# Another arena layout and another order of work ahead of the expert windows, in a two-layer decoder step

## The chip, the core and the metric

One core of one Trainium2 chip runs the whole step in one launch. The time is device microseconds of that core, from start to end of an execution. Three executions of the kernel before took 3319.91, 3323.1 and 3322.9 us.

## The reference, cut to what matters

512 prompt tokens and 8 new tokens, width 1024, go through two layers; all of it is float32.

```
layer 0: y = differential attention with ALiBi (8 heads; the 8 new tokens also see 2 cached pages each)
layer 1: y = gated short convolution
each layer: h = LN(alpha*h + y)
            q = h @ w_q; per head: scores against 2 x 128 keys, top 16 of each, top 16 of the 256 sums
            idx = 16 experts of 16384, g = softmax(top scores)      # 8 heads -> 128 experts per token
            a = u_tab[idx] . h;  h = LN(alpha*h + sum_k g*gelu(a) * v_tab[idx])
            h = h + sigmoid(h @ Wg) * (p @ Wp)
```

A token meets 128 experts in a layer. For a tile of 128 tokens one gather fetches, for each token, one expert's row of u and of v, 8 KB, so a gather is 1 MB, and there are 1040 of them (4 tiles of 128 and one short one, in two layers).

## The kernel before, in words

Each of the five engines runs its own program, written from one list of pieces of work that the class `Plan` makes; an engine's instructions stand in the order of that list, and nothing overtakes. First there is a long stretch without experts, the *lead*: queries and keys (L1538), the values (`v`, L1581), 32 units of scores and softmax (`score`, `weigh`, `w_turn`, `pv`), the attention of the new tokens over cached pages (`s_out`, `o_turn`), the norms of the heads (`ms0`, `rms0`, `ms1`, `rms1`), the output product (`mix`), the layer norm (`norm_a`, `norm_b`), its turn, the first query features (`pq`) and the routing of the first heads (`route`, four pieces for each head; the fourth writes the ids of 16 experts).

Then come windows, one for each tile of tokens: 32 steps of four experts. An expert passes from the gather (POOL, L912) into a slot of the arena, to its dot product (DVE, L1500), to the gate and the diagonal matrix (ACT, L1078 to L1088), to two additions into `acc` (PE, L1683), which free the slot. The arena has 11 slots of 8 KB per partition. What else is to be done (products, norms, the next tile's routing) is dealt out over the 32 steps by `window`, from a start step to an end step and by the numbers in COST. DVE and ACT do these pieces two half steps (BEHIND) later than PE.

Before the first gathers the arena holds the buffers of the attention. Slots 0 to 2 hold scores and softmax; slots 3 to 5 the values of the prompt and half of the attention's output (`oT_early`); 6 to 8 the new tokens' values and two pairs of cache pages (`kv_pages`); 9 and 10 the other half of the output, `s_rows` and `rstd8`. So POOL issues gathers 0 to 5 as soon as the ids are there, 6 to 8 once the last `s_out` is done, and 9 and 10 after the last `rms1` (L905 to L911).

Weights come as panels of 1 MB over SP's queue, in order, into two homes in turn; each waits until the panel before it in its home is used up. The pages of the cache come over POOL's queue, two pairs at a time, and a pair waits for the use of the one before it (`vpair_used`). The products of PE go through four banks; a product waits until its bank's last content was read. Pieces with `fence` wait for all banks.

## Time and profile before

| | |
|---|---|
| median of three executions | 3322.9 us (3319.91 to 3323.1) |
| the profiled execution | 3319.91 us, its span 3318.0 us |
| PE, DVE, ACT, POOL busy | 91%, 68%, 38%, 37% |
| moved by DMA | 1248.09 MB, 376 GB/s over the span |
| mean granted TensorE clock | 0.967 of 2.4 GHz |
| chain that ended last | PE 57%, DMA 16%, DVE 16% |

A stretch's row in the table of windows has the busy time of each engine with the number of its instructions, the granted clock of PE (1.00 is 2.4 GHz, 0.50 is 1.2 GHz), the busy share of the core's 16 DMA engines and what they moved. In rows of the timeline, what stands in brackets is the idle time ahead of the instruction and who ended it. The lead ends near 386 us, the first window runs to about 745 us, the second to about 1070 us.

### The profile page before, as it was taken

The page shows a single profiled execution, that of the slowest core. Times are in us where ns is not written, and L with a number is a line of the kernel's source. Part 1 is how long each engine was busy: PE and PEld are TensorE (multiplying, and loading weights), DVE is VectorE, ACT ScalarE, POOL GpSimd, SP SyncE. Part 2 cuts the span into 40 slices and gives each one's busy share as a digit, 9 for nine tenths or more (in the row PEclk, how much of TensorE's full clock was granted, in tenths as well). Part 3 has the DMA queues.
Part 4 walks back from the last instruction along what each step waited for, and adds up shares of the span by engine and source line. Part 5 has one row for each costly group of instructions (what it writes and reads, how often), then busy time and mean ns, then how long its engine had stood idle before and what let it go on. Part 6 is the DMA issues. An engine that isn't in the chain of part 4 may idle for free.

```text
span 3318.0 us, 33637 instructions
## 1 busy us (share of the span) xinstructions
PE 3010.6 (91%) x9426; PEld 1674.3 (50%) x9426; DVE 2250.1 (68%) x5801; ACT 1268.1 (38%) x3602; POOL 1241.6 (37%) x1100
## 2 busy tenths in 40 slices
PE   8998899789997899999898799999999788888888
PEld 7765555335563455654454355665455344443334
DVE  0653657877647877778768757764667888787454
ACT  0143333343423543333433464332434445435332
POOL 0100234443434334443344334444644435444431
PEclk9998799899999999999999899999999989999999
DMA  4513799999999999999899999999999999999997
GB/s 177 210 72 117 280 390 411 420 422 407 412 412 421 400 408 419 421 421 421 345 421 421 401 371 396 414 419 392 422 421 420 422 382 384 422 397 421 421 421 295
DMA packets 179819, 1248.09 MB, mean 376 GB/s; under 512 B 20087, under 2 KB 23415, under 8 KB 32433
## 3 DMA queue, kind: packets, MB, share of 16 engines
q0 software_dynamic: 156896, 1115.93, 82.2%
q1 hardware_dynamic: 22592, 128.97, 9.8%
q8 instruction: 75, 1.23, 0.1%
q10 hardware_dynamic: 144, 1.05, 0.1%
q14 instruction: 112, 0.91, 0.1%
HBM read 1239.41 MB, written 6.50 MB: 375 GB/s over the span
## 4 chain that ended last, share of the span: by engine, by line
PE 57%; DMA 16%; DVE 16%; ACT 4%; DVEq 3%; issue 3%; POOL 1%; ACTq 1%; POOLq 0%; SPq 0%
PE acc L1683 30%; DMA arena<-in_uv,idx 15%; PE bank L1709 10%; PE bank L1700 7%; DVE arena L1500 7%; PE bank L1538 3%; PE bank L1581 2%; DVEq L1408 2%; ACT diag L1088 1%; ACT L1072 1%; POOL arena L912 1%; DVE yb L1344 1%; DMA arena<-in_uv,small 1%; DVE ya L1343 1%; DVE ya L1354 1%
## 5 line engine op out<-in xcount | busy, mean ns | idle before, releaser
L1683 PE MATMUL acc<-arena,diag 128*128 128x512 f32 x4160 | 1935.0, 614 | 233.5 <-ACT diag L1088 228.4
L912 POOL DMA_INDIRECT arena<-in_uv,idx x1024 | 1194.5, 1166 | 1690.9 <-PE acc L1683 1560.5
L1500 DVE CUSTOM_DVE_ANT_0 arena<-arena,h 128x1024 f32<-128x1024 f32 x1024 | 1217.8, 1221 | 367.5 <-DMA arena<-in_uv,idx 364.4
L1683 PEld LDWEIGHTS acc<-arena,diag 128*128 128x128 f32 x4160 | 794.3, 196 | 1201.4 <-issue 840.9
L1078 ACT ACTIVATE act_w<-dots 128x2 f32<-128x2 f32 x520 | 105.3, 202 | 1382.9 <-DVE dots L1500 1382.3
L1088 ACT ACTIVATE diag<-cst,act_w 128x128 f32<-128x128 f32 x1040 | 370.0, 395 | 149.4 <-PE acc L1683 115.9
L1709 PE MATMUL bank<-hT,panel 128*128 128x264 f32 (+2 forms) x1792 | 403.4, 379 | 2.2 <-ACT hT L1045 2.2
L1709 PEld LDWEIGHTS bank<-hT,panel 128*128 128x128 f32 x1792 | 335.5, 190 | 97.6 <-issue 52.6
L1081 ACT ACTIVATE act_w<-act_w 128x1 f32<-128x1 f32 x1040 | 250.2, 287 | 43.4 <-issue 1.1
L1078 ACT ACT_TABLE_LOAD x128 | 164.2, 1283 | 1.6
L1700 PE MATMUL bank<-panel,hT 128*128 128x256 f32 (+1 forms) x576 | 131.8, 383 | 5.4 <-ACT hT L1045 5.4
L1700 PEld LDWEIGHTS bank<-panel,hT 128*128 128x128 f32 (+1 forms) x576 | 97.0, 170 | 49.0 <-issue 24.2
L1700 PE MATMUL bank<-panel,qT 128*128 128x256 f32 (+1 forms) x512 | 115.4, 379 | 0.0
L1700 PEld LDWEIGHTS bank<-panel,qT 128*128 128x128 f32 (+1 forms) x512 | 83.8, 165 | 38.6 <-issue 15.8
L1072 ACT ACT_TABLE_LOAD x80 | 102.6, 1283 | 1.4
L1337 DVE COPY yb<-tp 128x256 f32<-128x256 f32 x80 | 34.0, 425 | 97.7 <-PE tp L1667 92.7
L1415 DVE SCALAR_TENSOR_TENSOR h<-h,bank 128x256 f32<-128x256 f32 (+1 forms) x40 | 16.7, 419 | 106.3 <-PE bank L1700 104.9
L1500 DVE DVE_READ_ACCUMULATOR2_ANT dots<- 128x1 f32 x1040 | 85.1, 82 | 0.0
L1538 PE MATMUL bank<-keys,panel 128*128 128x256 f32 x256 | 60.9, 393 | 9.3 <-DMA panel<-in_panels 9.3
L1667 PEld LDWEIGHTS tp<-keys,qT 128*128 128x128 f32 (+1 forms) x320 | 43.3, 172 | 43.1 <-issue 42.0
L1053 ACT ACTIVATE qT<-bank 128x264 f32<-128x264 f32 (+2 forms) x68 | 24.8, 365 | 103.0 <-PE bank L1709 102.8
L1382 DVE TENSOR_TENSOR yb<-ya,cst 128x512 f32<-128x512 f32 x80 | 55.4, 693 | 11.4 <-issue 0.6
(201 smaller groups left out, 2169.1 us busy)
## 6 DMA issues: line engine op xcount, KB each, us to landing
panel<-in_panels SPq DMA_DIRECT2D x103, 1024.0 KB
arena<-in_uv,idx POOLq DMA_INDIRECT x1024
arena<-in_cache_k POOLq DMA_DIRECT2D x16, 512.0 KB, 5.5
arena<-in_cache_v POOLq DMA_DIRECT2D x16, 512.0 KB, 5.0
arena<-out_y_s POOLq DMA_DIRECT2D x8, 512.0 KB, 6.0
arena<-in_panels SPq DMA_DIRECT2D x4, 1024.0 KB, 8.1
lng<-in_ln SPq DMA_DIRECT2D x6, 512.0 KB
lnb<-in_ln SPq DMA_DIRECT2D x6, 512.0 KB
```

The lines of the kernel that those rows point to most:

```text
L912: nc.gpsimd.indirect_dma_start(uv[:, e % SLOTS_UV, :], None, uv_dram[layer], bass.IndirectOffsetOnAxis(ids[:, r:r + 1], 0)).then_inc(gathe ...
L1072: nc.scalar.activation(r_ex, r_tv, ACT.Exp, bias=r_nm, accum_out=r_sum).then_inc(gexp_done, 1)
L1078: nc.scalar.activation(act_w[:, 1, half, s], dots[:, half, s], ACT.Gelu).then_inc(gelu_done, 1)
L1081: nc.scalar.activation(act_w[:, 2, half, r:r + 1], act_w[:, 1, half, r:r + 1], ACT.Copy, scale=act_w[:, 0, half, r:r + 1])
L1088: nc.scalar.activation(diag[:, r % DIAGS, :], mask, ACT.Copy, scale=act_w[:, 2, half, r:r + 1]).then_inc(diag_ready, 1)
L1408: dve.drain()
L1500: V.tensor_tensor_reduce(uv[:, e % SLOTS_UV, 0:D], uv[:, e % SLOTS_UV, 0:D], x_rows, 1.0, 0.0, ALU.mult, ALU.add, dots[:, G % 2, r:r + 1]) ...
L1538: m = mm(pj[n % 2][:, PW + G_OFF[g]:PW + G_OFF[g] + G_W[g]], w[:, c, :], src[g][:, c, 0:G_W[g]], start=(c == 0), stop=(c == C - 1))
L1581: t = mm(product_of[0:m, 0:PW], src[group_of(x.b)][:, c, local(x.b):local(x.b) + m], w[:, c, :], start=(c == 0), stop=(c == C - 1))
L1683: m = mm(acc[:, half * 512:(half + 1) * 512], diag[:, r % DIAGS, :], uv[:, e % SLOTS_UV, D + half * 512:D + (half + 1) * 512], start=False ...
L1700: last = mm(bank[0:m, x.n % BANKS, 0:PW], src[:, c, local(x.b):local(x.b) + m], weights[:, c, :], start=(c == 0), stop=(c == chunks - 1))
L1709: last = mm(bank[:, x.n % BANKS, 0:width], w[:, c, :], hT[:, c, lo:lo + width], start=(c == 0), stop=(c == C - 1))
```

## The change

Four parts go together.

*Layout.* Slots 0 to 2 stay. Slots 3 and 4 now hold the late half of the output, `s_rows` and `rstd8`; all values, the early half of the output and the cache pages lie from slot 5 on. Gathers 0 to 2 need the ids alone, 3 and 4 wait for the last `rms1`, and 5 to 10 for the last product of the first `mix` (`last_mix`).

*Panels.* The third and fourth panel of the first `mix` get homes of their own in the room of the values, and are loaded once all sums of the attention and all stores of the values are done; they no longer wait for the first two panels.

*Order of the lead.* The key rows of the new tokens stand ahead of the first two products of values, and the fence moves to them. The second part of `s_out` comes one unit after the first instead of three units. `ms0` stands ahead of the last scores, without the Sqrt instruction that loaded the table early. The four `mix` products of tile 0 come together, `q[0:2]` and all of head 0's routing earlier; three `mix` products of tile 1 move to the end of the lead.

*Windows.* All of head 1's routing stands in the first window instead of three quarters of it in the lead. Heads 3 to 7 are dealt over steps 5 to 16 (before 5 to 20). The second group's `mix`, norm and turns move from the second window to steps 16 to 32 of the first, and its query features take steps 0 to 17 of the second window (before, both shared steps 0 to 23).

The diff, without the lines that only rename the value buffers:

```diff
--- before.py
+++ after.py
@@ -55,8 +55,7 @@
 FREE_AT_FIRST = 3
-HELD_BY_PAGES = 6
-HELD_BY_SAMPLE = 9
+FREE_NEXT = 5
@@ -151,7 +150,7 @@
-        once = {("pq", 0, 0): "queries"}
+        once = {("mix", 0, 2): "values0", ("mix", 0, 3): "values1", ("pq", 0, 0): "queries"}
         self.home, self.before, self.nth = [], [], []
@@ -181,8 +180,8 @@
         key_rows = [[product("k_rows", b=b, half=half) for half in range(2)] for b in range(BLOCKS)]
+        key_rows[TB][0].fence = True
         values = [[product("v", self.v_panels[p], p=p, b=b) for b in range(BLOCKS)] for p in range(4)]
-        values[0][0].fence = True
         score = [[product("score", u=u, half=c) for c in range(2)] for u in range(len(UNITS))]
@@ -202,8 +201,7 @@
         for b in range(TB):
-            if b >= 2:
-                fill[b - 1].append(values[0][b])
+            fill[b].append(values[0][b])
             for half in range(2):
@@ -214,11 +212,11 @@
         for k in range(4):
-            fill[24 + k + 2 * (k // 2)].append(out[k // 2][k % 2])
+            fill[25 + k].append(out[k // 2][k % 2])
         for k in range(2):
-            fill[24 + k] += square[2 * k:2 * k + 2]
-
-        lead = values[0][0:2] + key_rows[TB] + [Piece("s_new")]
+            fill[28 + k] += square[2 * k:2 * k + 2]
+
+        lead = key_rows[TB] + [Piece("s_new")]
         for t in range(len(UNITS) - 1):
@@ -391,7 +389,7 @@
         m1[0].fence = True
-        self.keys_after = m0[0].panel
+        self.keys_after = m0[2].panel
         a0, a1, c0, c1 = self.norm(0, GROUP_TILES[0], False, True)
@@ -399,30 +397,30 @@
         rms1 = [self.product(Piece("rms1", hd=hd)) for hd in range(HEADS)]
-        self.last_rms = rms1[-1]
+        self.last_mix, self.last_rms = m1[3], rms1[-1]
         self.ms0, self.ms1 = ms0, ms1
...
         roots = [Piece("root", i=g) for g in range(2)]
-        lead += score[31] + [weigh[30], turned[29], ms0, roots[0], turned[30], f0, weigh[31], summed[6, 1]] + rms0[0] \
-            + [turned[31], m0[0], summed[7, 1], m0[1], f1] + rms0[1] + [m1[0], o_turn[0], out[2][0], m1[1], out[2][1]] \
-            + [m0[2], m0[3], a0, m1[2], m1[3], c0] + t0 + q[0:2] + r[0:1] + q[2:4] + r[1:3] + out[3] + [o_turn[1]] + r[3:7] \
-            + [ms1, roots[1], f2] + rms1
+        lead += [ms0] + score[31] + [weigh[30], turned[29], roots[0], f0, turned[30], weigh[31], summed[6, 1]] + rms0[0] \
+            + [turned[31], m0[0], summed[7, 1], m0[1], o_turn[0], out[2][0], m0[2], m0[3], f1, a0] \
+            + rms0[1] + [out[2][1], c0, m1[0]] + t0 + [out[3][0]] + q[0:2] + r[0:4] + [out[3][1], o_turn[1]] + q[2:4] \
+            + [ms1, roots[1], f2] + rms1 + m1[1:4]
         steps = [("alone", 0, 0, [lead])]
-        early = r[7:8] + [a1, c1] + t1 + q[4:6] + late[0:2] + r[8:12] + late[2:4]
+        early = r[4:8] + [a1, c1] + t1 + q[4:6] + late[0:2] + r[8:12] + late[2:4]
         rest = q[6:8]
...
         r1 = self.route(0, 1)
-        window(0, 0, (0, 5, early), (5, 20, rest), (20, 32, r1[:17]))
-        bg, r2 = bg + self.features("pq", 0, 1), self.route(0, 2)
-        window(0, 1, (0, 8, r1[17:]), (20, 32, r2[:17]), (0, 23, bg))
+        window(0, 0, (0, 5, early), (5, 16, rest), (16, 32, r1[:21]), (16, 32, bg))
+        bg, r2 = self.features("pq", 0, 1), self.route(0, 2)
+        window(0, 1, (0, 8, r1[21:]), (17, 32, r2[:21]), (0, 17, bg))
...
         early, late = cut_at(bg, 0.56)
-        window(0, 2, (0, 8, r2[17:]), (8, 32, r3), (0, 32, early))
+        window(0, 2, (0, 6, r2[21:]), (6, 32, r3), (0, 32, early))
         side, spread = self.sample_rows(0)
@@ -604,26 +602,21 @@
-        v_flat = part(TB * D)
-        oT_early = part(C * G_W[0]).rearrange("p (c t) -> p c t", c=C)
-        assert at[0] <= HELD_BY_PAGES * 2 * D
-        at[0] = HELD_BY_PAGES * 2 * D
-
-        v_new = part(D)
-        kv_flat = part(4 * D)
-        assert at[0] <= HELD_BY_SAMPLE * 2 * D
-        at[0] = HELD_BY_SAMPLE * 2 * D
-
-        oT_late = part(C * G_W[1])
+        oT_late = part(C * G_W[1]).rearrange("p (c t) -> p c t", c=C)
         s_rows = part(D)
         rstd8 = part(G_W[0] + G_W[1])[0:HEADS, :]
-        v_rows = [v_flat[:, b * D:(b + 1) * D] for b in range(TB)] + [v_new]
-        oT = [oT_early, oT_late.rearrange("p (c t) -> p c t", c=C)]
+        assert at[0] <= FREE_NEXT * 2 * D
+        at[0] = FREE_NEXT * 2 * D
+
+        v_flat = part(BLOCKS * D)
+        v_rows = v_flat.rearrange("p (b n) -> p b n", b=BLOCKS)
+        oT = [part(C * G_W[0]).rearrange("p (c t) -> p c t", c=C), oT_late]
         oT_normed = [oT[0], qT[:, q_off[1]:q_off[1] + C * G_W[1]].rearrange("p (c t) -> p c t", c=C)]
+        kv_flat = part(4 * D)
         kv_pages = kv_flat.rearrange("p (i j n) -> p i j n", i=2, j=2)
...
-        q_all = oT_late[:, 0:2 * D].rearrange("p (i n) -> p i n", i=2)
+        q_all = logit_flat[:, 0:2 * D].rearrange("p (i n) -> p i n", i=2)
         wl = wT_flat[:, 0:4 * HD]
@@ -631,7 +624,7 @@
         q_free = q_off[1] + C * G_W[1]
-        homes = {0: panel[:, 0, :], 1: panel[:, 1, :], "queries": qT[:, q_free:q_free + 2 * D]}
+        homes = {0: panel[:, 0, :], 1: panel[:, 1, :], "values0": v_flat[:, 0:2 * D], "values1": v_flat[:, 2 * D:4 * D], "queries": qT[:, q_free:q_free + 2 * D]}
         k_new = x_sample
@@ -796,8 +789,9 @@
                     sp.wait_ge(full if kind == "pair" else bank_full, count)
-                elif home == "queries":
+                elif home in ("values0", "values1", "queries"):
                     sp.wait_ge(a_o, len(SUMS))
+                    sp.wait_ge(v_out, 16 * BLOCKS)
                 sp.dma_start(panel_of(i), panels[PANEL_AT[plan.panels[i]]]).then_inc(s_panel[home], 16)
@@ -905,10 +899,10 @@
                         pool.wait_ge(slot_done, e - SLOTS_UV + 1)
-                    elif e == HELD_BY_PAGES:
-                        pool.wait_ge(bank_full, plan.sample_out[3][1].n + 1)
-                    elif e == HELD_BY_SAMPLE:
+                    elif e == FREE_AT_FIRST:
                         read(pool, plan.last_rms)
+                    elif e == FREE_NEXT:
+                        pool.wait_ge(bank_full, plan.last_mix.n + 1)
                     nc.gpsimd.indirect_dma_start(
@@ -1017,7 +1011,6 @@
                 elif x.kind == "ms0":
-                    nc.scalar.activation(small[:, 61:62], eps, ACT.Sqrt)
                     act.drain()
@@ -1569,14 +1562,14 @@
                     m = rows(x.b)
+                    if x.fence:
+                        all_read(pe, len(ORDER))
                     for k in range(4):
...
                     m, w = rows(x.b), panel_of(x.panel).rearrange("p (c n) -> p c n", c=C)
-                    if x.fence:
-                        all_read(pe, len(ORDER))
                     for c in range(C):
```

The start of PE's work on values and scores. L1581 (after: L1574) is a product of values, eight matmuls each, L1573 (L1568) the turn of key rows, those with 8 rows being of the new tokens, L1586 (L1579) a half of a unit's scores. Before:

```order
L1581 MATMUL bank<-panel,keys 128x256 x16
L1573 MATMUL bank<-cst,qT 8x128 x8
L1586 MATMUL bank<-qT 128x128 x2
L1573 MATMUL bank<-cst,qT 128x128 x4
L1586 MATMUL bank<-qT 128x256 x2
```

After:

```order
L1568 MATMUL bank<-cst,qT 8x128 x8
L1579 MATMUL bank<-qT 128x128 x2
L1574 MATMUL bank<-panel,keys 128x256 x8
L1568 MATMUL bank<-cst,qT 128x128 x4
L1579 MATMUL bank<-qT 128x256 x2
```

Two products of values stood ahead of the new tokens' key rows; now none does, and one stands behind the first unit's scores.

PE at the end of the lead, from the last `mix` product of tile 0 on: L1731 (L1724) turns tile 0, L1629 and L1634 (L1622, L1627) are the last parts of `s_out`, L1709 (L1702) query features, L1667 (L1660) key scores of a head, L1557 (L1550) is `ms1`, L1654 (L1647) `rms1`. Before:

```order
L1700 MATMUL bank<-panel,arena 128x256 x32
L1731 MATMUL bank<-cst,h 128x128 x8
L1709 MATMUL bank<-hT,qT 128x128 x16
L1667 MATMUL tp<-keys,qT 128x128 x2
L1709 MATMUL bank<-hT,panel 128x128 x16
L1629 MATMUL bank<-arena,x_sample 32x512 x4
L1634 MATMUL bank<-arena,x_sample 32x512 x2
L1629 MATMUL bank<-arena,x_sample 32x512 x4
L1634 MATMUL bank<-arena,x_sample 32x512 x2
L1639 MATMUL bank<-cst,arena 128x4 x8
L1667 MATMUL tp<-keys,qT 128x128 x2
L1557 MATMUL bank<-hT,cst 8x264 x8
```

After:

```order
L1724 MATMUL bank<-cst,h 128x128 x8
L1622 MATMUL bank<-arena,x_sample 32x512 x4
L1627 MATMUL bank<-arena,x_sample 32x512 x2
L1702 MATMUL bank<-hT,qT 128x128 x16
L1660 MATMUL tp<-keys,qT 128x128 x2
L1622 MATMUL bank<-arena,x_sample 32x512 x4
L1627 MATMUL bank<-arena,x_sample 32x512 x2
L1632 MATMUL bank<-cst,arena 128x4 x8
L1702 MATMUL bank<-hT,panel 128x128 x16
L1550 MATMUL bank<-hT,cst 8x264 x8
L1647 MATMUL bank<-arena,cst 128x264 x8
L1693 MATMUL bank<-panel,arena 128x256 x8
```

The first of the last two parts of `s_out` now stands ahead of the first query features, and a `mix` product of tile 1 (with two more behind it) behind `rms1`.

DVE at the opening of the first window: L1500 (L1493) is a dot product, L1337 to L1377 (L1330 to L1370) the search for a head's best keys, L1393 (L1386) writes its ids, L1300 (L1293) ends the norm of tile 1. Before, from the last of the lead:

```order
L1377 CAST ya<-ya 128x32
L1245 RECIPROCAL arena<-arena 8x264
L1419 SCALAR_TENSOR_TENSOR qT<-arena,small,bank 128x264 x8
L1500 ISA arena,dots<-arena,h 128x1024
```

After, behind the first four dots:

```order
L1493 ISA dots 128x1
L1330 COPY yb<-tp 128x256
L1333 MAX ya<-yb 128x8 x2
L1336 MAX_INDEX ya<-ya,yb 128x8
L1337 MATCH_REPLACE yb<-ya,yb 128x128
```

The search for head 1 stood ahead of the first dot; it now stands behind the fourth, ahead of the fifth.

## Rows read from the trace of the kernel before

**Rows 1.** Table of windows, five stretches: columns as told above

```profile
402.00:445.00 43.00, 40.06 (x165) 25.29 (x166) 26.63 (x69) 15.28 (x49) 18.08 (x14) 1.00 0.92 342
445.00:500.00 55.00, 55.00 (x160) 30.48 (x160) 29.77 (x63) 17.28 (x64) 21.41 (x19) 0.97 1.01 422
500.00:510.00 10.00, 10.00 (x35) 6.37 (x34) 9.11 (x26) 4.87 (x12) 2.75 (x2) 1.00 0.88 346
760.00:1010.00 250.00, 245.87 (x789) 141.10 (x787) 155.24 (x346) 89.85 (x276) 101.44 (x88) 0.99 1.01 410
830.00:840.00 10.00, 10.00 (x24) 4.18 (x22) 9.41 (x16) 7.89 (x14) 6.86 (x6) 1.00 0.95 374
```

**Rows 2.** Timeline of PE, start of the values: start, us, instruction

```profile
127.48 7.14 PE L1581 MATMUL bank<-panel,keys 128*128 128x256 f32 x32 [0.89 <-ACT qT L956]
134.46 1.04 PE L1573 MATMUL bank<-cst,qT 128*8 128x128 f32 x8
...
140.13 0.70 PE L1586 MATMUL bank<-qT 64*128 64x256 f32 x2 [3.00 <-DVE small L1220]
```

**Rows 3.** Timeline of DVE, the same stretch

```profile
133.31 0.21 DVE L1161 TENSOR_SCALAR small<-small,arena 128x1 f32<-128x1 f32 x1
135.10 1.28 DVE L1254 COPY x_sample<-bank 8x512 f32<-8x512 f32 x2 [1.58 <-PE bank L1573]
...
139.78 0.29 DVE L1220 CUSTOM_DVE_ANT_0 arena<-bank,pTs 128x128 f32<-128x128 f32 x1
```

**Rows 4.** Timeline of PE, end of the attention

```profile
252.61 1.91 PE L1629 MATMUL bank<-arena,x_sample 128*32 128x512 f32 x8
...
265.10 3.31 PE L1629 MATMUL bank<-arena,x_sample 128*32 128x512 f32 x8 [2.54 <-DMA arena<-in_cache_v]
...
276.77 1.13 PE L1586 MATMUL bank<-qT 64*128 64x512 f32 x4
...
284.17 2.79 PE L1557 MATMUL bank<-hT,cst 128*8 128x256 f32 x8 [3.33 <-ACT hT L963]
...
289.62 2.05 PE L1649 MATMUL bank<-arena,cst 8*128 8x128 f32 x16
```

**Rows 5.** Timeline of POOL: a page load, the first gather, a late one

```profile
255.83 0.55 POOL L875 DMA_DIRECT2D arena<-in_cache_v  x1 [10.21 <-issue]
...
363.22 1.00 POOL L912 DMA_INDIRECT arena<-in_uv,idx  x1 [32.41 <-DVE idx L1393]
...
394.12 0.94 POOL L912 DMA_INDIRECT arena<-in_uv,idx  x1 [3.42 <-PE acc L1683]
...
506.94 0.94 POOL L912 DMA_INDIRECT arena<-in_uv,idx  x1 [12.09 <-DVE idx L1393]
```

**Rows 6.** Timeline of PE, second half of the lead

```profile
297.87 3.62 PE L1700 MATMUL bank<-panel,arena 128*128 128x256 f32 x16
...
306.13 6.75 PE L1700 MATMUL bank<-panel,arena 128*128 128x256 f32 x16 [1.18 <-DVE arena L1273]
...
352.37 3.74 PE L1709 MATMUL bank<-hT,panel 128*128 128x128 f32 x32
...
367.97 6.57 PE L1557 MATMUL bank<-hT,cst 128*8 128x264 f32 x16 [1.53 <-ACT hT L963]
378.26 7.37 PE L1654 MATMUL bank<-arena,cst 8*128 8x264 f32 x16 [3.73 <-DVE arena L1245]
```

**Rows 7.** Timeline of DVE, head 0's routing to the first window

```profile
352.57 0.42 DVE L1337 COPY yb<-tp 128x256 f32<-128x256 f32 x1 [9.95 <-PE tp L1667]
...
358.42 0.14 DVE L1370 TENSOR_SCALAR ya<-ya 128x1 f32<-128x1 f32 x1
...
362.17 0.18 DVE L1393 SCALAR_TENSOR_TENSOR idx<-ya 128x16 int32<-128x16 f32 x1
...
386.36 1.22 DVE L1500 CUSTOM_DVE_ANT_0 arena<-arena,h 128x1024 f32<-128x1024 f32 x1 [0.20 <-issue]
...
400.73 1.28 DVE L1300 SCALAR_TENSOR_TENSOR h<-h,rstd,lnb 128x1024 f32<-128x1024 f32 x1
```

More of the change, by code:

```diff
@@ L897, in _ @@
                 dst = nv_p[b * P:(b + 1) * P, :] if b < TB else nv_s
-                pool.dma_start(dst, v_rows[b][0:rows(b), :]).then_inc(v_out, 16)
+                pool.dma_start(dst, v_rows[0:rows(b), b, :]).then_inc(v_out, 16)
             for i in range(NS + 2, 2 * NS):
@@ L977, in lead @@
                     m = rows(x.b)
-                    nc.scalar.activation(v_rows[x.b][0:m, x.p * PW:(x.p + 1) * PW], product_of[0:m, 0:PW],
+                    nc.scalar.activation(v_rows[0:m, x.b, x.p * PW:(x.p + 1) * PW], product_of[0:m, 0:PW],
                                          ACT.Copy).then_inc(bank_free[x.n % BANKS], 1)
@@ L1633, in lead @@
                     for b in two:
-                        m = mm(product_of[b % 4 * 32:b % 4 * 32 + 32, :], s_weight_new[0:NS, b, :], v_new[0:NS, cols],
+                        m = mm(product_of[b % 4 * 32:b % 4 * 32 + 32, :], s_weight_new[0:NS, b, :], v_rows[0:NS, TB, cols],
                                start=False, stop=True)
```

2 lines of the change are left out of this document (1 added, 1 removed).

## The prediction, on record before the changed kernel ran

> **What bounds the kernel now.** I read the table of windows first. From 445 us on the DMA engines are full: share 1.01 and 422 GB/s, with PE busy the whole time [rows 1]. A gather is 1.05 MB, so at 422 GB/s the engines need 2.49 us for it, and the 1040 gathers alone take 2590 us. The change moves no byte more or less. The end can therefore move in two ways only: the stretch in which the DMA engines are full begins at another time, or they idle more or less inside it. Before 445 us there is a run-up: 402 to 445 us moves 342 GB/s with PE busy 40.06 of 43 us at full clock [rows 1], so there the additions, which free slots, set the pace of the gathers. Whatever delays them in the run-up delays everything behind it. Next I read the timelines of PE, DVE and POOL through the lead, which sets when the run-up begins: first gather 363.22, first dot 386.36, end of tile 1's norm 402.0 (400.73 + 1.28) [rows 5, 7]. The last is my marker: the turn of tile 1 waits for that norm, and in both orders the third pair of additions stands behind that turn.
>
> **Start of the values.** Now PE does two products of values in 7.14 us, then the new tokens' key rows [rows 2]. DVE is busy with the cache pages until 133.5 and copies the key rows at 135.10; its logits come at 139.78, and PE waits 3.00 us for them [rows 2, 3]. With the key rows first, PE is through them and the first scores (1.0 + 0.5) near 129.1. The next product of values takes the bank of the key rows, which DVE can copy only from 133.5 (0.7 us): PE stands still from 129.1 to 134.2. Then a product (3.6), key rows (0.4), and the second unit's scores, whose banks DVE frees at about 138.5, so 0.3 us more. Idle 5.4 against 3.0: **+2.4 us** (bounds 0, and 5.4 if a product behind the idle time runs at half clock). PE is gapless almost everywhere until 250, so this stays.
>
> **Pages for `s_out`.** The second part needs pages that are loaded when the first part is done: matmuls end at 254.5 (252.61 + 1.91), the loads are issued from 255.83, the next part begins at 265.10, 10.6 us later [rows 4, 5]. Work of three units lay between, and PE still idled 3.1 us (2.54 and 0.5). Now there is one unit, 3.9 us by the same rows' neighbours: 10.6 - 3.9 = 6.7 idle, **+3.7 us** (0 if the softmax would have made PE wait anyway, 3.7 if not; I take 3.7 since PE had no such wait over 0.5).
>
> **`ms0` ahead of the last scores.** Before, last scores at 276.77, `ms0` idles 3.33 for the squares, `rms0` at 289.62: 12.85 us [rows 4]. Now ms0 is done some 4 us after it starts, but the last scores start later by as much, and the logits, exponentials and weights of the last units lie between them and the head factors on DVE. Adding them up, 11.8: **-1.0** (-3.3 to +1). The early table load only changes its place. Sum to here **+5.1**.
>
> **From there to the first window.** Before, from `rms0` at 289.62 to the first dot 96.7 us. The new order, without the shift: `rms0` and the first `mix` to 296.5, then sum, `mix`, o_turn, s_out to 306.3; the two `mix` whose panels no longer wait to 313.3; head factors 316.8; s_out 319.7 (its matmuls end 318.7); `mix` 323.2, turn 324.3. Then PE meets the last cache pages: 318.7 + 10.6 = 329.3, idle 5.0, where before it met none. Part of s_out 332.2, features (3.74 to 6.0) [rows 6] 336 to 338, routing. From the copy of the scores to the ids DVE needs 9.8 us (352.57 to 362.17+0.18) [rows 7]: ids at 346 to 349, plus the shift of 5.1. So **the first gather comes at 352 to 355 instead of 363.22**, but only three go; eight wait for `rms1` and the last `mix`. Meanwhile ACT, in order, holds the head's exponential (top scores 5.9 us after the copy) ahead of the copy that o_turn needs: PE idles 4 to 5 us again. Features, then from the start of `ms1` to the end of `rms1` 17.6 us (367.97 to 385.6) [rows 6]: 368 to 374. Three `mix` products: 10.5 us at 2.4 GHz; 306.13 shows one taking 6.75 instead of 3.62 after short waits [rows 6], so up to 20. First dot at 379 to 394, middle 385.5: **-1** (-7.5 to +8), before the shift.
>
> **Head 1's routing.** Before, three quarters of it ran on DVE in the lead while PE did `ms1`. Now 7.4 us of it stands between the fourth dot and the fifth, with the norm of tile 1 behind: before, first dot to end of the norm 15.7 us (386.36 to 402.0) [rows 7], now 23.6. **+7.9** (0 if something else ends last there, 7.9 if not; PE reaches the turn in any case before). The marker moves from 402 to about 414: +5.1 - 1 + 7.9 = **+12**.
>
> **Inside the full stretch.** POOL waits 12.09 us for head 3's ids at 506.94, and the share falls to 0.88, 346 GB/s [rows 1, 5]. Head 3 is now about one step earlier: **-1.3** (share) to -1.8 (rate). From 760 to 1010 `mix`, norm and query features share 23 steps; a step with 1.5 products costs PE 6.9 + 5.2 us, more than four gathers and half a panel cost the DMA engines (9.96 + 1.3). The rate is 410 [rows 1]: 250 x 11/421 = 6.5 us. By the share it is far less (0.95 in the worst ten microseconds [rows 1], 1.01 over the whole), so most of the lower rate is traffic of another kind that stays. I take **-2** (-1 to -6.5). In the new first window the steps 5 to 32 carry about one product each; PE 10.9, DMA 10.9 us: no new loss (0 to +4: DVE has 4 dots of 1.22 and some 5 us of routing in a step, 90% of it).
>
> **Sum.** +12 - 1.3 - 2 = +8.7. The profiled execution took 3319.91 us (span 3318.0 and 1.9 around it): 3328.6 for such a one. It lies 3.0 below the median of 3322.9, so against the median 3331.6; I say 3331.
>
> **Rivals.** *A: the head start counts (faster).* Five gathers, 12.5 us of transfer, can be done before the window opens. If the additions catch up in the run-up, as PE's 3 us idle in 402 to 445 and the missing 79 GB/s (8 us) there [rows 1] allow, the first gather's 8 to 11 us are kept: -8 - 1.3 - 2 = -11, 3312. Against it: only 11 slots exist, the twelfth gather waits for an addition as at 394.12 [rows 5], and that addition waits for the first window. It decides if the twelfth gather comes before 394. Chance 0.2.
>
> *B: half clock and waits add up (slower).* After the page wait and the ACT wait the features, `ms1`, `rms1` and the last `mix` run at 1.2 GHz, the first dot comes at 394 + 5: the lead adds +20, in all +17: 3340. For it: 6.75 instead of 3.62 at 306.13 [rows 6]. Chance 0.2. [...]
>
> *C: nothing that counts moves (same).* The first page wait falls where PE would wait for the softmax (-3.7), and the losses at 500 and in 760 to 1010 come back whole, by the rate: 12 - 3.7 - 1.8 - 6.5 = 0, 3323. For it: the rate of 410 [rows 1], and PE idles little in the units, so that little is known of what would end last there. Against it: the share. Chance 0.25.
>
> **How the numbers follow.** Forecast 0.35, A 0.2, B 0.2, C 0.25. 0.2% is 6.6 us, about what a measurement of this kernel tells from no change. Slower: B, and four fifths of the forecast: 0.48. Faster: A and a little of C: 0.22. Same: 0.30. The forecast's own range is 3322 to 3338; for 8 in 10 it reaches to near A and B: 3314 to 3343.
>
> **What would show it.** In the profile after: PE idle near 5 us at the first product of values, waiting for DVE; a page wait of 6 to 7 us in the second part of `s_out` and of about 5 us ahead of the first query features; first gather at 352 to 355, three alone, the sixth not before the last `mix`; first dot near 390; end of tile 1's norm near 414; full DMA from about 457; no wait of 12 us for head 3's ids. Wrong if the norm ends before 405, or if the DMA engines are full before 445.

## The result: slower, by about three times what was forecast

The kernel after takes 3346.4 us (median of four executions, 3342.7 to 3351.1) against 3323.0 for the one before: a ratio of 1.0074 [1.0056, 1.0091]. The forecast was +8.7 us and slower; it is +23.4. The sign was right, the size and the range (up to 3343) were not. The profiled execution has a span of 3341.6 us, 23.6 more than before; as before, it moves 1248.09 MB.

The page's rows of 40 slices and the heads of its parts 1 and 4, of the kernel after:

```profile
PE 3011.3 (90%) x9426; PEld 1674.9 (50%) x9426; DVE 2249.6 (67%) x5801; ACT 1269.3 (38%) x3601; POOL 1226.2 (37%) x1100
...
GB/s 176 208 93 104 199 365 421 396 421 400 420 421 421 405 406 419 421 421 421 331 421 421 420 358 395 412 416 395 419 421 420 421 391 378 422 393 421 421 421 304
...
PE 54%; DMA 17%; DVE 17%; ACT 4%; DVEq 4%; issue 3%; POOL 1%; ACTq 1%; POOLq 0%; SPq 0%
```

From the seventh slice (501 us) most slices stand at 421 GB/s: the cap that the prediction built on is still there, and the question is when it starts. The table of windows of the kernel after, in the columns of [rows 1]:

```profile
402.00:445.00 43.00, 32.73 (x108) 19.30 (x109) 27.81 (x69) 15.24 (x43) 15.15 (x14) 0.80 0.88 343
424.00:465.00 41.00, 39.67 (x158) 24.46 (x156) 21.78 (x60) 13.38 (x40) 16.15 (x14) 0.97 0.85 312
465.00:500.00 35.00, 33.55 (x106) 20.84 (x107) 19.25 (x34) 11.72 (x43) 13.78 (x11) 0.95 1.01 416
600.00:650.00 50.00, 46.35 (x141) 23.68 (x140) 39.42 (x107) 17.05 (x56) 18.64 (x16) 0.93 0.96 380
760.00:1010.00 250.00, 229.31 (x681) 124.54 (x680) 154.51 (x361) 89.62 (x289) 102.18 (x95) 1.00 1.01 414
```

```profile
244.38:300.84 56.46, 42.17 (x164) 17.80 (x163) 22.32 (x87) 23.45 (x66) 4.87 (x9) 0.82 0.32 113
268.00:277.00 9.00, 8.90 (x22) 1.99 (x24) 1.10 (x5) 0.98 (x2) 0.00 (x0) 0.50 0.00 0
421.00:428.00 7.00, 7.00 (x15) 3.48 (x16) 7.00 (x13) 3.13 (x12) 1.61 (x1) 0.59 0.70 288
```

And from the kernel before, the stretch that answers to the first of the second fence (the end of the attention up to `rms0`):

```profile
244.34:289.62 45.28, 38.22 (x163) 16.93 (x162) 23.18 (x88) 23.08 (x67) 4.76 (x9) 0.89 0.46 164
```

I come back to the stretches of the last two fences. The share reaches 1.01 only from 465 us, where before it did from 445 [rows 1]: 20 us later. Nearly all of the 23.4 us was lost by then.

**Where the lateness arises.** I compared the same events in both timelines. This is PE of the kernel after, from the start of the values to the last `rms0` of the first group; L1574 is a product of values, L1622 the products of `s_out`, L1598 softmax times values, L1550 `ms0`, L1642 `rms0`:

```profile
126.67 1.03 PE L1568 MATMUL bank<-cst,qT 128*8 128x128 f32 x8 [0.89 <-ACT qT L950]
...
133.53 2.05 PE L1574 MATMUL bank<-panel,keys 128*128 128x256 f32 x4 [5.40 <-DVE x_sample L1247]
...
235.89 2.42 PE L1574 MATMUL bank<-panel,hT 128*128 128x256 f32 x10
...
250.33 0.55 PE L1587 MATMUL tp<-cst,arena 128*128 128x128 f32 x3 [2.25 <-DVE arena L1230]
...
256.08 1.91 PE L1622 MATMUL bank<-arena,x_sample 128*32 128x512 f32 x8
...
268.10 3.62 PE L1622 MATMUL bank<-arena,x_sample 128*32 128x512 f32 x8 [6.72 <-DMA arena<-in_cache_v]
...
286.70 1.60 PE L1598 MATMUL acc<-arena 128*128 128x256 f32 x4 [2.87 <-ACT arena L988]
...
297.22 0.90 PE L1587 MATMUL tp<-cst,arena 128*128 128x128 f32 x3 [2.45 <-DVE arena L1230]
297.92 2.99 PE L1598 MATMUL acc<-arena 128*128 128x256 f32 x8
300.84 2.05 PE L1642 MATMUL bank<-arena,cst 8*128 8x128 f32 x16
```

And two rows of the kernel before, the same place at 235 us and a last unit's softmax times values:

```profile
235.85 2.42 PE L1581 MATMUL bank<-panel,hT 128*128 128x256 f32 x10
...
275.60 0.92 PE L1605 MATMUL acc<-arena 128*128 128x256 f32 x4 [0.21 <-ACT arena L994]
```

PE stands still 5.40 us at the first product of values, as forecast, and yet both kernels are level at 235.9. A wait of 2.25 us for DVE at 250.33 is new: before, the first part of `s_out` stood in its place. Then comes the page wait, 6.72 us for 2.54 in [rows 4]. Eight matmuls behind it take 3.62 us where the same form took 1.91 at 256.08: the granted clock of 268 to 277 us is 0.50 of 2.4 GHz, so 1.2 GHz (table above). Then PE waits 2.87 us for an exponential of ACT, where before it waited 0.21, and 2.45 us for DVE, each with slow matmuls behind it (L1598 with 4 takes 1.60 for 0.92). `rms0` is 11.2 us late (300.84, 289.62 in [rows 4]). The two rows of windows divide it: from 244.4 us on PE is idle 14.3 us for 7.1 before, and busy 42.2 for 38.2 with almost the same matmuls. So 7.2 us are waits and 4.0 are matmuls at the lower clock.

The second half, PE, DVE, ACT and POOL of the kernel after, one fence for each:

```profile
346.19 1.91 PE L1622 MATMUL bank<-arena,x_sample 128*32 128x512 f32 x8 [1.66 <-DMA arena<-in_cache_v]
...
362.31 3.54 PE L1632 MATMUL bank<-cst,arena 128*128 128x4 f32 x16 [4.46 <-issue]
...
420.96 1.09 PE L1724 MATMUL bank<-cst,h 128*128 128x128 f32 x4 [10.27 <-DVE h L1293]
421.84 6.03 PE L1676 MATMUL acc<-arena,diag 128*128 128x512 f32 x8
```

```profile
398.16 1.23 DVE L1493 CUSTOM_DVE_ANT_0 arena<-arena,h 128x1024 f32<-128x1024 f32 x1 [0.20 <-issue]
...
402.92 0.42 DVE L1330 COPY yb<-tp 128x256 f32<-128x256 f32 x1
...
419.53 1.28 DVE L1293 SCALAR_TENSOR_TENSOR h<-h,rstd,lnb 128x1024 f32<-128x1024 f32 x1
```

```profile
361.08 0.31 ACT L1065 ACTIVATE ya<-ya 128x16 f32<-128x16 f32 x1 [5.69 <-DVE ya L1363]
...
361.50 0.59 ACT L1003 ACTIVATE arena<-bank 64x512 f32<-64x512 f32 x1
```

```profile
366.17 1.00 POOL L906 DMA_INDIRECT arena<-in_uv,idx  x1 [25.07 <-DVE idx L1386]
...
385.52 0.94 POOL L906 DMA_INDIRECT arena<-in_uv,idx  x1 [15.84 <-DVE qT L1412]
...
397.77 0.94 POOL L906 DMA_INDIRECT arena<-in_uv,idx  x1 [10.07 <-PE bank L1693]
```

The marker, the end of tile 1's norm, lies at 420.8 (419.53 + 1.28), 18.8 later than before: 11.2 up to `rms0`, 0.6 from there to the first dot (398.16 - 300.84 = 97.3, before 96.7), and 7.0 from the first dot to the end of the norm (22.65, before 15.7), where the copy of head 1's scores at 402.92 opens its search. PE then meets the turn after 10.27 us of waiting, and its eight matmuls of additions take 6.03 us (granted clock 0.59 from 421 to 428). At the same place before it waited 2.90 and they took 3.60. So from the 17th gather on POOL is 21.6 us late.

Each gather's issue can be set against the one of the same number before. The lateness is 21.6 us at the 17th and 33rd, 17.8 at the 49th (head 3's ids: no wait for them is left), 33 to 41 between the 81st and the 177th, where `mix` and the norms of the second group now come earlier (its four panels, 4 MB, are 10 us of this rise at 421 GB/s, the rest I did not trace), 21.3 at the 225th, 24.6 at the 449th, 25.1 at the last. The last 3.8 us can't be put down to the change, as the next section shows.

### The profile page after: what moved, and what is told of

Its sections match the earlier page's. It is cut to its first block, busy times and chain, and to the rows that moved or that the text cites. A ratio compares the mean times of both kernels' runs of the same rounds, so it can differ in the third digit from the quotient of the medians.

```text
span 3341.6 us, 33639 instructions
## 1 busy us (share of the span) xinstructions
PE 3011.3 (90%) x9426; PEld 1674.9 (50%) x9426; DVE 2249.6 (67%) x5801; ACT 1269.3 (38%) x3601; POOL 1226.2 (37%) x1100
## 2 busy tenths in 40 slices
DMA packets 179818, 1248.09 MB, mean 373 GB/s; under 512 B 20086, under 2 KB 23414, under 8 KB 32432
## 4 chain that ended last, share of the span: by engine, by line
PE 54%; DMA 17%; DVE 17%; ACT 4%; DVEq 4%; issue 3%; POOL 1%; ACTq 1%; POOLq 0%; SPq 0%
PE acc L1676 29%; DMA arena<-in_uv,idx 15%; PE bank L1702 10%; PE bank L1693 7%; DVE arena L1493 7%; PE bank L1574 2%; DVEq L1401 2%; PE bank L1531 2%; ACT diag L1081 1%; ACT L1065 1%; POOL arena L906 1%; DMA arena<-out_y_s 1%; DVE ya L1336 1%; PE bank L1579 1%; DVE yb L1337 1%
## 5 line engine op out<-in xcount | busy, mean ns | idle before, releaser
L906 POOL DMA_INDIRECT arena<-in_uv,idx x1024 | 1176.9, 1149 | 1722.5 <-PE acc L1676 1609.1
L1493 DVE CUSTOM_DVE_ANT_0 arena<-arena,h 128x1024 f32<-128x1024 f32 x1024 | 1217.2, 1220 | 349.2 <-DMA arena<-in_uv,idx 346.3
L1702 PE MATMUL bank<-hT,panel 128*128 128x264 f32 (+2 forms) x1792 | 406.9, 381 | 3.8 <-ACT hT L1038 3.8
L1702 PEld LDWEIGHTS bank<-hT,panel 128*128 128x128 f32 x1792 | 338.1, 192 | 100.1 <-issue 55.0
L1693 PEld LDWEIGHTS bank<-panel,hT 128*128 128x128 f32 (+1 forms) x576 | 96.9, 170 | 49.1 <-issue 24.3
L1330 DVE COPY yb<-tp 128x256 f32<-128x256 f32 x80 | 34.0, 425 | 98.7 <-PE tp L1660 93.4
L1493 DVE DVE_READ_ACCUMULATOR2_ANT dots<- 128x1 f32 x1040 | 84.0, 81 | 0.0
L1392 DVE RECIPROCAL ya<-ya 128x1 f32<-128x1 f32 x80 | 13.0, 162 | 81.1 <-ACT ya L1065 81.1
L1660 PEld LDWEIGHTS tp<-keys,qT 128*128 128x128 f32 (+1 forms) x320 | 43.0, 170 | 43.7 <-issue 42.6
```

What stands on the lines that cost most here:

```text
L906: nc.gpsimd.indirect_dma_start(uv[:, e % SLOTS_UV, :], None, uv_dram[layer], bass.IndirectOffsetOnAxis(ids[:, r:r + 1], 0)).then_inc(gathe ...
L1493: V.tensor_tensor_reduce(uv[:, e % SLOTS_UV, 0:D], uv[:, e % SLOTS_UV, 0:D], x_rows, 1.0, 0.0, ALU.mult, ALU.add, dots[:, G % 2, r:r + 1]) ...
L1693: last = mm(bank[0:m, x.n % BANKS, 0:PW], src[:, c, local(x.b):local(x.b) + m], weights[:, c, :], start=(c == 0), stop=(c == chunks - 1))
L1702: last = mm(bank[:, x.n % BANKS, 0:width], w[:, c, :], hT[:, c, lo:lo + width], start=(c == 0), stop=(c == C - 1))
```

## The experiments

Twelve kernels. "Before" is the kernel before, timed beside each on the same chip.

| | time, us | before | ratio |
|---|---|---|---|
| e1 after, `s_out` back | 3336.7 | 3320.5 | 1.0045 [1.003, 1.0059] |
| e2 after, `ms0` back | 3345.9 | 3320.5 | 1.007 [1.0056, 1.0084] |
| e3 after, head 1 back | 3342.7 | 3320.5 | 1.006 [1.0045, 1.0074] |
| e4 before + windows | 3323.3 | 3320.5 | 1.0006 [0.9997, 1.0015] |
| e5 before + held gathers | 3325.6 | 3321.6 | 1.001 [1.0001, 1.0019] |
| e6 before + `s_out` order | 3331.3 | 3321.6 | 1.0031 [1.0018, 1.0043] |
| e7 before + head 1 in the window | 3329.5 | 3321.6 | 1.0021 [1.0012, 1.003] |
| e8 after, `s_out` and tail back | 3325.7 | 3320.7 | 1.0017 [1.0008, 1.0027] |
| e9 e6, PE kept busy | 3327.9 | 3320.7 | 1.0023 [1.0013, 1.0032] |
| e10 before, second part later | 3317.5 | 3320.7 | 0.9989 [0.998, 0.9998] |
| e11 before, `mix` order | 3320.0 | 3320.7 | 0.9998 [0.9989, 1.0007] |
| e12 e10 + heads 3 to 7 by step 16 | 3314.5 | 3323.4 | 0.9978 [0.9969, 0.9986] |

How far can one timeline be trusted? e4, e5 and e7 run the program of before as far as the first gather, and their profiled executions reach `rms0` at 288.59, 287.74 and 288.12 us (before 289.62) and the first gather at 362.11, 359.40 and 361.67 (before 363.22); e3, with the program of after, has `rms0` at 303.62 (after 300.84). An event's lateness is therefore sure to some 2 to 3 us at `rms0` and 4 us at the first gather. Behind the 225th gather all kernels but e12 lose 2.0 to 5.2 us against before up to the last gather, e5 (2.3) and e11 (3.0) among them, which change nothing there. I put that loss down to the one profiled execution of before and read nothing from it.

### The order of `s_out`: e1, e6, e9, e10

e1, in the kernel after:

```diff
-            fill[25 + k].append(out[k // 2][k % 2])
+            fill[24 + k + 2 * (k // 2)].append(out[k // 2][k % 2])
```

> The changed kernel with the four parts of s_out back in their old units (24, 25, 28, 29); all else as changed. Theory T (the end moves with the additions' progress at the opening of the first window, set by PE and DVE in the lead): the 6.7 us page wait in the second part shrinks to 2 to 4 us, PE keeps the full clock behind it, and of the 11 us that the end of the attention lost 6 to 9 come back; 3337 to 3341 us against 3346. Rival G (the end moves with the number of gathers done before the window, eight of which are held back): the page wait is hidden by other waits, at most 2 us come back, 3344 to 3346.

e6 is the same line the other way round, in the kernel before.

> The kernel before with the four parts of s_out in units 25 to 28, as in the changed kernel; all else as before. Theory T: the page wait grows from 2.5 to about 6.7 us and PE falls to 1.2 GHz behind it, 5 to 9 us slower: 3328 to 3332. Rival (the loss needs ms0 ahead of the last scores): 0 to 3 us slower, 3323 to 3326.

PE of e6:

```profile
250.12 0.55 PE L1594 MATMUL tp<-cst,arena 128*128 128x128 f32 x3 [2.24 <-DVE arena L1237]
...
252.79 2.75 PE L1629 MATMUL bank<-arena,x_sample 128*32 128x512 f32 x8
...
269.63 3.63 PE L1629 MATMUL bank<-arena,x_sample 128*32 128x512 f32 x8 [6.87 <-DMA arena<-in_cache_v]
...
286.15 0.92 PE L1605 MATMUL acc<-arena 128*128 128x256 f32 x4 [2.27 <-ACT arena L994]
...
300.06 2.05 PE L1649 MATMUL bank<-arena,cst 8*128 8x128 f32 x16
```

Its row of windows for the stretch up to `rms0`:

```profile
244.17:300.06 55.89, 40.84 (x163) 16.82 (x162) 23.21 (x88) 23.30 (x67) 4.75 (x9) 0.82 0.37 133
```

e6 costs 9.6 us (3331.3 - 3321.6). e1 gives back about as much: 1.0074 - 1.0045 of 3322 us is 9.6 (7.2 by the medians' distance to before), and its last gather comes 11.8 us earlier than in the kernel after (13.3 late for 25.1). The line explains some 40% of the result.

The wait is only 4.3 us longer (6.87 for 2.54 in [rows 4]), but `rms0` is 10.4 us late. What is the rest? In the stretch up to `rms0` both kernels run the same 163 matmuls, before in 45.28 us and e6 in 55.89. Of the 10.6 us between them 8.0 are idle time (15.05 for 7.06) and 2.6 are slower matmuls (40.84 for 38.22). The idle time has three parts: 4.3 for the pages; 2.1 for ACT's exponential (2.27 for 0.21), presumably since the units' scores now follow each other with less of `s_out` between them; and 1.7 net at the start, where the first part of `s_out` no longer covers a wait of 2.24 us for DVE (250.12), while one of 0.52 for ACT is gone.

e9 keeps the page wait's place filled with work: in e6, 15 products of a constant with a constant (30 matmuls in the trace) go into the bank ahead of the wait.

```diff
+                    if x.part == 1 and x.half == 0:
+                        for _ in range(15):
+                            mm(product_of[:, 0:256], const("ident"), cst[:, 0:256], start=True, stop=True)
                     pe.wait_ge(s_weighted, 1)
```

> The kernel before with s_out in units 25 to 28, as in the run with the pages alone (3331.25, 9.6 us slower), and with 15 matmuls of 256 columns that compute nothing, on the free bank, in the place where PE waits for the pages: the wait stays, PE is busy in it. Theory H (some 5 of the 9.6 us are work at half clock behind the wait): the clock stays high and the time falls to 3324 to 3327. Rival P (the wait itself and the later softmax are the price, the clock nothing): 3330 to 3333.

PE of e9:

```profile
262.91 6.74 PE L1624 MATMUL bank<-cst 128*128 128x256 f32 x30
270.10 1.91 PE L1632 MATMUL bank<-arena,x_sample 128*32 128x512 f32 x8 [0.44 <-DMA arena<-in_cache_v]
...
282.48 0.92 PE L1605 MATMUL acc<-arena 128*128 128x256 f32 x4 [2.27 <-ACT arena L994]
...
296.38 2.05 PE L1652 MATMUL bank<-arena,cst 8*128 8x128 f32 x16
```

The pages still come when they come (270.10), but the products behind them take 1.91 us, and `rms0` is reached 3.7 us earlier than in e6. So the lower clock behind the page wait costs e6 some 3.7 us in the timeline. In time e9 costs 7.2 us (3327.9 - 3320.7) for e6's 9.6, 2.4 less, but the intervals overlap (4.3 to 10.6 and 6.0 to 14.3 us), so that by the times alone the clock's part is not shown. Nor do 3.7 and 2.6 contradict each other: the kernel before has matmuls at half clock here too (3.31 for 1.91 in [rows 4]), and 2.6 is what e6 has beyond that.

e10 goes further than the kernel before did: the second part comes a unit later still.

```diff
-            fill[24 + k + 2 * (k // 2)].append(out[k // 2][k % 2])
+            fill[24 + k + 3 * (k // 2)].append(out[k // 2][k % 2])
```

> The kernel before with the second part of s_out one unit later (29 and 30 instead of 28 and 29), so four units after the first; all else as before. Theory T: the wait of 2.5 us for the pages and the half clock behind it (3.31 instead of 1.91) go, 2 to 5 us faster: 3316 to 3319. Rival: the softmax units end last there and take the place of the wait, no change, 3320 to 3322.

```profile
264.80 1.91 PE L1629 MATMUL bank<-arena,x_sample 128*32 128x512 f32 x8 [0.57 <-DMA arena<-in_cache_v]
...
286.25 2.04 PE L1649 MATMUL bank<-arena,cst 8*128 8x128 f32 x16
```

The wait of 2.54 is 0.57, the products take 1.91 for 3.31 [rows 4], and `rms0` comes 3.4 us earlier than in before's profile (1.5 to 2.3 earlier than in those of e4, e5 and e7). The kernel is 3.2 us faster, with an interval from 0.7 to 6.6. Its gathers are 6.1 to 6.5 us early up to the 225th and 3.4 at the last. This is no head start given back in the windows: up to 3.8 us of it lie in the execution, as the first gathers of e4, e5 and e7 show, and the loss behind the 225th is the one of all kernels told above.

### `ms0` ahead of the last scores: e2

```diff
-        lead += [ms0] + score[31] + [weigh[30], turned[29], roots[0], f0, turned[30], weigh[31], summed[6, 1]] + rms0[0] \
+        lead += score[31] + [weigh[30], turned[29], ms0, roots[0], turned[30], f0, weigh[31], summed[6, 1]] + rms0[0] \
```

> The changed kernel with ms0 again behind the last scores (the early table load stays away); all else as changed. Theory T: in the profile after, the last scores start 4 us after ms0 begins and the softmax of the last unit hangs on them, so 2 to 4 us come back: 3342 to 3344. Rival C (all of the 11 us is the page wait and the half clock behind it): no change, 3345 to 3347.

A ratio of 1.007 [1.0056, 1.0084] against 1.0074 [1.0056, 1.0091]: no difference that can be measured, and theory T's 2 to 4 us did not come back.

### Head 1's routing: e7 and e3

e7, in the kernel before (head 1's four pieces all go to the first window):

```diff
-            + ... + [o_turn[1]] + r[3:7] \
+            + ... + [o_turn[1]] + r[3:4] \
-        early = r[7:8] + [a1, c1] + ...
+        early = r[4:8] + [a1, c1] + ...
```

> The kernel before with all of head 1's routing but none of its quarter pieces in the lead, that is, all four pieces in the first window, behind the fourth dot; all else as before. Theory T: the norm of tile 1 ends 7 us later, PE waits 10 us for it and does the next additions at 1.2 GHz, 8 to 10 us slower: 3331 to 3333. Rival G: no gather starts later, since head 1's ids are needed only from gather 16 on, 0 to 2 us: 3323 to 3325.

DVE of e7:

```profile
383.49 1.23 DVE L1500 CUSTOM_DVE_ANT_0 arena<-arena,h 128x1024 f32<-128x1024 f32 x1 [0.20 <-issue]
...
395.32 1.22 DVE L1500 CUSTOM_DVE_ANT_0 arena<-arena,h 128x1024 f32<-128x1024 f32 x1
...
404.85 1.28 DVE L1300 SCALAR_TENSOR_TENSOR h<-h,rstd,lnb 128x1024 f32<-128x1024 f32 x1
```

The fifth dot (395.32) waits until the search is over, and the norm ends 22.6 us after the first dot (before 15.7). PE waits 11.96 us for it at the turn, 4.89 in e4. The first dot is 2.9 us earlier than before, but so it is by 2.3 in e4, whose lead is that of before; that taking the search away makes it earlier is not shown. The kernel is 7.9 us slower.

e3 puts the pieces back into the lead of the kernel after, behind its late `q[2:4]`.

```diff
-            + ... + [out[3][1], o_turn[1]] + q[2:4] \
+            + ... + [out[3][1], o_turn[1]] + q[2:4] + r[4:7] \
-        early = r[4:8] + [a1, c1] + ...
+        early = r[7:8] + [a1, c1] + ...
```

> The changed kernel with the first three quarters of head 1's routing back in the lead, between the last early query features and ms1; all else as changed. Theory T: DVE idles 10.5 us there, so the pieces are hidden; the norm of tile 1 ends 7 us earlier and PE does not wait 10.3 us at half clock for it, 7 to 10 us come back: 3336 to 3339. Rival G: no gather starts earlier, so nothing comes back, 3345 to 3347.

PE of e3:

```profile
385.61 7.38 PE L1647 MATMUL bank<-arena,cst 8*128 8x264 f32 x16 [5.38 <-DVE arena L1238]
...
422.64 1.09 PE L1724 MATMUL bank<-cst,h 128*128 128x128 f32 x4 [4.75 <-DVE h L1293]
```

This miss taught most. It gains 1 to 5 us (1.2 by the medians' distance to before, 4.6 by the ratios), not the 8 of e7, and the turn of tile 1 is no earlier (422.64 for 420.96). In the order of after there is no PE work left beside the search but `ms1`: DVE comes late to the head factors, and PE idles 5.38 us ahead of `rms1`. From `rms0` to the first dot it takes 103.4 us (97.3 in the kernel after), from there to the end of the norm 15.4 (22.65): most of the eight are paid ahead of the first dot instead of behind it.

### The gathers held back: e5

In the kernel before, gathers 3 to 5 wait for the last `rms1` as well; those behind them stand in the same queue.

```diff
+                    elif e == FREE_AT_FIRST:
+                        read(pool, plan.last_rms)
                     elif e == HELD_BY_PAGES:
```

> The kernel before with gathers 3 to 8 held until the last rms1 is done (a further wait at gather 3), so that only three go ahead of the first window, as in the changed kernel; all else as before. Theory T: the dots of experts 3 to 7 come some us later but the norm of tile 1 is what the additions wait for, so 0 to 5 us slower: 3323 to 3328. Rival G: six gathers of 2.49 us fewer are done before the window, 12 to 18 us slower: 3335 to 3341.

DVE of e5:

```profile
385.83 1.23 DVE L1502 CUSTOM_DVE_ANT_0 arena<-arena,h 128x1024 f32<-128x1024 f32 x1 [3.31 <-DMA arena<-in_uv,idx]
```

3.9 us slower, with an interval from 0.3 to 6.3 us. The timeline shows where: after three dots DVE waits 3.31 us for the first of the held gathers to land, and from the first dot (378.99) to the end of the norm (397.81) it takes 18.8 us, 15.7 before. In the kernel after this wait does not exist: the fourth gather is issued at 385.52, 12.6 us ahead of the first dot, and the first four dots follow each other at 1.15 us. So the price of e5 must not be added to the kernel after.

### The windows: e4, and the whole lead: e8

e4 is the kernel before with the changed `window` lines, of which this is the first:

```diff
-        window(0, 0, (0, 5, early), (5, 20, rest), (20, 32, r1[:17]))
+        window(0, 0, (0, 5, early), (5, 16, rest), (16, 32, r1[:21]), (16, 32, bg))
```

> The kernel before with the changed windows alone (steps 5 to 16, the second group's mix in the first window, its features in steps 0 to 17 of the second); lead and layout as before. Theory T: the lag between the two profiles is 21.65 us at the 16th gather and 24.8 later, so the windows cost nothing or up to 3 us: 3320 to 3326. The rival W that the denser windows starve the DMA engines (share 0.96 at 600 to 650, 0.98 at 750 to 800 in the profile after): 5 us or more slower, 3328 to 3333.

+2.9 us, not distinguishable from nothing. Its gathers are 0.7 us early at the 33rd, 4.6 at the 49th (no wait for head 3's ids) and 0.7 again at the 225th: what the windows gain at head 3's ids they give back.

e8 undoes, in the kernel after, `s_out`'s order (the line of e1) and the order of the tail (below); layout, panels and windows stay.

```diff
-            + ... + t0 + [out[3][0]] + q[0:2] + r[0:4] + [out[3][1], o_turn[1]] + q[2:4] \
+            + ... + t0 + [out[3][0]] + q[0:2] + r[0:1] + q[2:4] + r[1:3] + [out[3][1], o_turn[1]] + r[3:7] \
-        early = r[4:8] + [a1, c1] + ...
+        early = r[7:8] + [a1, c1] + ...
```

> The changed kernel with two things back: the parts of s_out in units 24, 25, 28, 29, and the tail's order of features and routing (head 0's later pieces behind the features q[2:4], so that ACT's exponential doesn't stand ahead of the copy that o_turn needs, and three quarters of head 1's routing before ms1). Layout, panels, start, ms0 and windows as changed. Theory T, by the one-part runs (pages 9.7, head 1 7.9 us): 3346 - 18 = 3328, and 3324 if the 4.5 us idle of PE at o_turn goes as well. Rival S (the layout and the windows hold the rest, and what comes back at the tail is given back at the late gathers): 3333 to 3337.

PE of e8:

```profile
352.67 1.95 PE L1632 MATMUL bank<-cst,arena 128*128 128x4 f32 x16 [0.69 <-ACT arena L1003]
...
400.07 1.08 PE L1724 MATMUL bank<-cst,h 128*128 128x128 f32 x4 [3.06 <-DVE h L1293]
```

With these two orders back, the kernel is 5.0 us above before instead of 23.4: they carry 18 to 19 us. The turn of tile 1 is reached at 400.07, level with e4's 399.79 (before 402.16), and the wait for ACT is 0.69 instead of 4.46. Its gathers are 0.9 us late at the 17th and 0.5 at the 225th, and its first four dots follow each other without a wait, so the held gathers cost nothing here either. Where the 5.0 us (2.7 to 9.0) that are left lie, is not shown; the windows of e4 are the nearest candidate.

### Towards a faster kernel: e11 and e12

e11, in the kernel before, puts the head factors ahead of the second `mix` and the last sum.

```diff
-            + [turned[31], m0[0], summed[7, 1], m0[1], f1] + rms0[1] + [m1[0], o_turn[0], out[2][0], m1[1], out[2][1]] \
+            + [turned[31], m0[0], f1, summed[7, 1], m0[1]] + rms0[1] + [o_turn[0], m1[0], out[2][0], m1[1], out[2][1]] \
```

> The kernel before with the head factors f1 computed one step earlier on DVE and o_turn ahead of the mix product that reads what DVE has just scaled; all else as before. Theory T: waits of 1.45 and 1.18 us go and the product that took 6.75 us takes 3.6, which shifts the additions 4 to 6 us: 3315 to 3318. Rival: the panel for the next product, loaded when this one is done, and the norm of tile 0 end last, so 0 to 2 us: 3319 to 3322.

No difference that can be measured; theory T had 4 to 6 us. PE's wait of 1.45 us is gone, but the `mix` product that took 6.75 us still takes 6.29 (at 307.22), behind a wait of 0.48. e12 is e10 with one number of the changed windows, the one that takes away the wait for head 3's ids.

```diff
-        window(0, 0, (0, 5, early), (5, 20, rest), (20, 32, r1[:17]))
+        window(0, 0, (0, 5, early), (5, 16, rest), (20, 32, r1[:17]))
```

> The kernel before with the second part of s_out at units 29 and 30 (3317.5 us alone) and heads 3 to 7 dealt over steps 5 to 16 of the first window instead of 5 to 20; mix, norms and features of the second group stay in the second window. Theory T: head 3's ids come before gather 48 wants them, the DMA idle time there (1.3 to 1.8 us) goes, and in the profile of the windows-only run the lag fell by 3.9 us at gather 48: 3313 to 3316. Rival: the denser steps 5 to 16 take it back by gather 144, as the windows-only run did later: 3317 to 3319.

Windows and POOL of e12:

```profile
500.00:510.00 10.00, 8.80 (x26) 4.61 (x26) 9.18 (x25) 3.27 (x11) 5.22 (x5) 1.00 1.01 421
```

```profile
354.94 1.00 POOL L912 DMA_INDIRECT arena<-in_uv,idx  x1 [32.47 <-DVE idx L1393]
```

The first gather comes 8.3 us earlier than in [rows 5], the share at 500 us is 1.01 instead of 0.88 [rows 1], and the last gather is 8.2 us early. At 3314.5 us it is faster than both kernels: 0.22% below the kernel before beside it. Its interval overlaps e10's, so the second line's own gain is likely and not shown.

## Why the prediction was right in sign and wrong in size

**The step that failed** is the sum of the first half of the lead, "+5.1" up to `rms0`; it was 11.2. Its term "+3.7" for the pages sized the wait rightly (6.72 for 6.7 forecast) and took the wait to be the whole cost. The line costs 9.6 us in e6, 7 to 12 in e1. What stood behind it, by e6's row of windows: 2.6 us more of matmuls at the lower clock, 2.1 us of another wait, for ACT's exponential, and 1.7 us net at the wait for DVE that the first part of `s_out` had covered. The kernel after shows the same kinds, 7.2 us of waits and 4.0 of slower matmuls. The working had the row for the clock: [rows 4] show the very form at 3.31 us behind a wait of 2.54 and at 1.91 ahead of it. I used half clock as a bound for the start of values and as a rival for the tail, and put none behind the one wait that I was surest of.

The Trainium skill (TensorE: Matmul & The Clock Gate, HAM oscillation) tells of a kernel in which the wait for the next load sends the array back to the lower clock each time, so that every group of matmuls starts slow. The trace agrees behind the waits of 6.72, 2.87 and 2.45 us; behind the wait of 1.66 us at 346.19 the products take 1.91 us, so not every wait does it. Nor does its length alone decide: behind the wait of 2.25 us at 250.33 the kernel after keeps the full clock (granted clock 1.00 from 252 to 255), and behind the same wait in e6 the products take 2.75 us for 1.91.

The others, one by one:

- *Start of the values, +2.4.* The idle 5.40 is there (5.4 forecast), the cost is not: PE enters the stretch 0.8 us earlier (126.67 for 127.48 in [rows 2]) and is level at 235.9. Over all kernels the place is passed at 234.0 to 235.9 with either order. Measured 0, the lower bound.
- *`ms0`, -1.0.* Measured 0 (e2), within some 5 us.
- *From `rms0` to the first dot, -1.* The middle of the working's own 379 and 394 is 386.5, not 385.5, so by its numbers the term was 0. Measured +0.6. That this is so near is luck, since the parts were off in both directions: the page wait was 1.66 us, not 5; the wait for ACT's exponential was 4.46, as forecast; the first gather came at 366.17, not at 352 to 355. 6 of these 11 to 14 us are the larger shift, and half clock stands behind the rest: from 303 to 344 us the granted clock is 0.79, and the products of `mix` and the parts of `s_out` there take some 8 us longer than the same forms at full clock. It changed nothing: three gathers alone, the fourth at 385.52 behind `rms1`, the sixth at 397.77 behind `mix`, as forecast.
- *Head 1's routing, +7.9.* Measured 7.0 in the timeline and 7.9 in e7. The one large term that was right in mechanism and size, though the working names 7.4 us of routing and doesn't say where the other 0.5 comes from.
- *Behind the marker*, a term that was missing: PE's wait of 10.27 us for the norm, with the turn and eight additions at half clock behind it, 2.8 us (18.8 at the marker, 21.6 at the 17th gather).
- *Held gathers*, costed at nothing: +3.9 [0.3, 6.3] in e5, but nothing in the kernel after, where they have landed before their dots.
- *Windows, -1.3 and -2.* The gain at head 3's ids was larger (3.9 us in the timeline, 21.6 to 17.8). But what moved out of 760 to 1010 us, where the rate rose only from 410 to 414 GB/s, went to 600 to 650, where it is 380. All in all e4 measured +2.9 [-1, +5] for -3.3; between the 33rd and the 225th gather its timeline shows 0 and that of the kernel after -0.3 (21.6 to 21.3). So the -3.3 did not come.

The forecast missed 14.7 us (23.4 - 8.7). By the timelines 9.6 of them lie ahead of the 17th gather: 6.1 in the first half of the lead, 1.6 from there to the first dot, -0.9 at the search, 2.8 behind the marker. 3.0 are the windows' gain that did not come, and the last 2.1 are within what executions differ by. By the experiments, 9.6 (`s_out`) + 7.9 (head 1) + 2.9 (windows) = 20.4 of 23.4, each uncertain by 3 to 4 us; e5's 3.9 would make it 24.3, but that is a wait which the kernel after doesn't have.

**The rivals.** A (the head start counts) fell: the twelfth gather came at 406.52, not before 394. C fell too: the page wait was not hidden, and nothing came back in the windows. B (half clock and waits add up, 3340) was nearest, and right in kind; its place was wrong. It looked for the half clock behind the page wait and the ACT wait, from the features on, and put the first dot at 399, of which 5 were the shift. The dot came at 398.16, near that by luck: 11.2 of it are the shift, and only 0.6 came behind `rms0`. The half clock that counted was at the end of the attention and at the turn of tile 1. B and the terms' upper bounds were set beside each other, though nothing excludes them together: B's 3340, with 5.4 for 2.4 at the start of the values and the 4 us of loss that I allowed the first window, reaches 3347, and 3346.4 is inside. That would have been the right range and still not the right account, for the first of these terms measured 0.
